# Gate and up projections of the dense layer: seven block products in place of eight for 20 of 22 column tiles

## The reference

```python
def swiglu(hn, w_gu, w_down):
    gte, up = jnp.split(hn @ w_gu, 2, axis=-1)
    return (jax.nn.silu(gte) * up) @ w_down
```

## Time and profile before

| | |
|---|---|
| Median of 3 runs | 1522.55 us (1520.13 to 1527.19) |
| The profiled execution | 1524.27 us, span of its instructions 1522.5 us |
| Granted TensorE clock, mean | 0.966 |
| TensorE busy | 1423.7 us, 94% |
| VectorE busy | 898.6 us, 59% |
| ScalarE busy | 639.4 us, 42% |
| GpSimd busy | 239.1 us, 16% |
| Gate and up of the dense layer | from 458.9 us to 713.4 us |
| Down projection of the dense layer | from 713.4 us to 840.1 us |

### The profile page before, as it was taken

How to read it: one execution, slowest core, us unless ns; L and a number is a source line. 1 busy time by engine, 2 the same in 40 slices (tenths; PEclk the granted TensorE clock), 3 DMA queues, 4 the chain that set the end, 5 groups by cost and what they waited for, 6 DMA issues and landing times. The chain is left out here.

```text
span 1522.5 us, 31277 instructions
## 1 busy us (share of the span) xinstructions
PE 1423.7 (94%) x12955; PEld 1264.7 (83%) x12955; DVE 898.6 (59%) x1196; ACT 639.4 (42%) x1076; POOL 239.1 (16%) x243
## 2 busy tenths in 40 slices
PE   7999999999899999999999997879599999999994
PEld 6999988888799999999999997559566777777772
DVE  5677536865755444444444756553547777677776
ACT  4444534441333222222233522662536556565661
POOL 0111016764120000000111101330140000000002
PEclk8999999999999999999999998899789999999997
DMA  6677422001523323332324540005267888888886
GB/s 185 211 287 264 132 77 52 2 3 31 180 85 107 87 83 100 93 83 70 100 82 133 148 107 32 1 18 150 76 200 257 294 282 294 293 287 274 273 285 236
DMA packets 170201, 226.47 MB, mean 149 GB/s; under 512 B 11544, under 2 KB 135089, under 8 KB 170009
## 3 DMA queue, kind: packets, MB, share of 16 engines
q1 hardware_dynamic: 160246, 191.44, 40.4%
q0 software_dynamic: 8976, 30.88, 5.7%
q10 hardware_dynamic: 862, 2.50, 0.5%
HBM read 188.78 MB, written 38.28 MB: 149 GB/s over the span
## 5 line engine op out<-in xcount | busy, mean ns | idle before, releaser
L281 DVE TENSOR_TENSOR w_lo<-w_raw,w_hi 128x2048 fp32r<-128x2048 f32 (+1 forms) x70 | 151.6, 2171 | 95.7 <-ACT w_hi L273 95.7
L226 PE MATMUL P<-xf_hi,w_hi 128*128 128x260 f32 x704 | 199.0, 283 | 2.0 <-DVEq L1857 1.2
L226 PE MATMUL P<-xf_hi,w_lo 128*128 128x260 f32 x704 | 198.9, 283 | 0.0
L226 PE MATMUL P<-xf_lo,w_hi 128*128 128x260 f32 x704 | 198.3, 282 | 0.0
L273 ACT ACTIVATE w_hi<-w_raw 128x2048 fp32r<-128x2048 f32 (+1 forms) x71 | 128.1, 1810 | 126.2 <-PE P L226 114.7
L226 PE MATMUL P<-xa_hi,w_hi 128*128 128x260 f32 x512 | 146.0, 285 | 5.3 <-DVE xa_lo L324 5.3
L226 PE MATMUL P<-xa_hi,w_lo 128*128 128x260 f32 x512 | 145.8, 285 | 0.0
L226 PE MATMUL P<-xa_lo,w_hi 128*128 128x260 f32 x512 | 145.4, 284 | 0.0
L226 PEld LDWEIGHTS P<-xf_hi,w_hi 128*128 128x128 f32 x704 | 132.5, 188 | 2.6 <-issue 1.4
L226 PEld LDWEIGHTS P<-xf_hi,w_lo 128*128 128x128 f32 x704 | 132.4, 188 | 0.0
L226 PEld LDWEIGHTS P<-xf_lo,w_hi 128*128 128x128 f32 x704 | 132.4, 188 | 0.0
(11 more groups left out here) (562 smaller groups left out, 3421.4 us busy)
## 6 DMA issues: line engine op xcount, KB each, us to landing
raw_more_moe<-in_moe_w_gu_dram SPq DMA_DIRECT2D x64, 512.0 KB, 5.4
w_raw<-in_moe_w_gu_dram SPq DMA_DIRECT2D x64, 512.0 KB, 6.1
w_raw<-in_dense_w_gu_dram SPq DMA_DIRECT2D x44, 512.0 KB, 5.1
expert_out<-zeros POOLq DMA_DIRECT2D x40, 512.0 KB, 4.2
w_raw<-in_a_w_in_dram SPq DMA_DIRECT2D x32, 512.0 KB, 5.0
raw_more_moe<-in_moe_w_down_dram SPq DMA_DIRECT2D x32, 512.0 KB, 4.8
w_raw<-in_moe_w_down_dram SPq DMA_DIRECT2D x32, 512.0 KB, 4.8
w_raw<-in_dense_w_down_dram SPq DMA_DIRECT2D x16, 384.0 KB, 3.9
```

The costliest lines, as they stand in the source:

```text
L226: ins = nc.tensor.matmul(out[:, b], w, x[:, b * HALF:(b + 1) * HALF], start=(first and n == 0), stop=(last and n == 2))
L281: ins = nc.vector.tensor_tensor(lo, raw, hi.bitcast(F32), ALU.subtract)
```

## The change

For tiles 2 to 21 the block product of weights and tokens is made with seven products in place of eight (Winograd's form of Strassen's scheme). The blocks of the weights are: A11 and A12, the gate columns of the first and last four feature blocks, A21 and A22 the same of the up columns. The tokens are split in four too: first and last four feature blocks, first and second half of the tokens. A weight block is 128 x 512. Four of the seven products take sums of weight blocks, S1 = A21 + A22, S2 = S1 - A11, S3 = A21 - A11 and S4 = A12 - S2, and four take sums of token blocks, which are made once. A product is 4 (blocks) x 3 = 12 matmuls of 260 columns in a bank of its own, so a tile takes 84. What each engine now does for a tile:

- GpSimd makes the four sums of the next tile's weights (`sums`), and multiplies `scratch` by `rstd` (`scale_up`).
- ScalarE casts seven pieces of 512 columns to `w_hi` (`high_piece`), each as soon as TensorE has used the same piece of the tile before, and copies the first bank out.
- VectorE makes seven `w_lo` pieces (`low_piece`) and, between them, seven additions of 260 columns that put gate and up together from the banks (`add`).
- Once, at the start: VectorE makes the token sums from `h` (`sum_tokens`), ScalarE their high parts, VectorE their low parts (`low_sum`). The high parts are put where `h` lies, so SyncE writes `h` out to memory first (`h_rows`) and reads it back behind the last product (`restored`), ahead of the rest of the down weights.

The core of the diff:

```diff
+    ORDER = ("A11", "S2", "S3", "S1", "A12", "A22", "S4")
...
         def _(sp):
+            sp.dma_start(h_rows, c.h[:].rearrange("p k t -> p (k t)")).then_inc(spilled, 16)
             st_gu.rest(c, sp)
             st_down.start(c, sp)
+            sp.wait_ge(used, all_used)
+            sp.dma_start(c.h[:].rearrange("p k t -> p (k t)"), h_rows).then_inc(restored, 16)
             st_down.rest(c, sp)
...
+            def sums(i, j):
+                pool.wait_ge(*loaded_of(i, j))
...
+                pool.wait_ge(piece_lo, piece_of(i, j, 3))
+                nc.gpsimd.tensor_tensor(to["S1"], a21, a22, ALU.add).then_inc(sums_made, 1)
+                pool.wait_ge(sums_made, count(1))
+                nc.gpsimd.tensor_tensor(to["S2"], to["S1"], a11, ALU.subtract).then_inc(sums_made, 1)
+                nc.gpsimd.tensor_tensor(a21, a21, a11, ALU.subtract).then_inc(sums_made, 1)
+                pool.wait_ge(sums_made, count(2))
+                pool.wait_ge(piece_lo, piece_of(i, j, 6))
+                nc.gpsimd.tensor_tensor(to["S4"], a12, to["S2"], ALU.subtract).then_inc(sums_made, 1)
+
+            def scale_up(i, j):
+                pool.wait_ge(read, read_of(i, j, 6))
+                nc.gpsimd.tensor_tensor(L.sf[:, j], L.sf[:, j], inward.rstd, ALU.mult).then_inc(up_read, 1)
+
+            sums(0, 1)
+            with pool.Fori(1, NFF // 2 - 1) as i:
+                for j in range(2):
+                    sums(i, j)
+                    scale_up(i, j)
...
+            def seven(i, j, first=False):
+                for q, name in enumerate(sv.ORDER):
+                    pe.wait_ge(piece_lo, piece_of(i, j, q))
...
+                    if q == 0:
+                        pe.wait_ge(first_copied, i * 2 + j)
+                    else:
+                        pe.wait_ge(read, read_of(i, j, (1, 2, 4, 5, 6, 7)[q - 1], -1))
...
+                    for k in range(4):
+                        for n, (w, x) in enumerate(((w_hi, x_hi), (w_hi, x_lo), (w_lo, x_hi))):
+                            ins = pe.matmul(c.P[:, q, 0:HALF], w[:, k], x[:, k], start=(k == 0 and n == 0), stop=(k == 3 and n == 2))
+                    ins.then_inc(used, 1)
...
+            def gu(i, j, last=False):
+                act.wait_ge(used, used_of(i, j, 0))
+                nc.scalar.activation(part(L.sg[:, j], 0), c.P[:, sv.bank("A11"), 0:HALF], ACT.Copy).then_inc(first_copied, 1)
...
+                    for q in range(pieces):
+                        high_piece(i, j, q, (used, used_of(i, j, q)))
+                    chunk_done(i, j)
+                silu(i, j)
+                f_high(i, j)
...
+            def gu(i, j, last=False):
...
+                low(0)
+                dve.wait_ge(first_copied, i * 2 + (j + 1))
+                add(i, j, 1, sv.one, gates[0], bank(1))
+                low(1)
...
+                add(i, j, 2, sv.three, sv.one, bank(2))
+                low(2)
...
+                add(i, j, 3, ups[1], sv.three, bank(3))
+                add(i, j, 3, gates[1], sv.one, bank(3))
+                low(3)
+                add(i, j, 4, gates[0], gates[0], bank(4))
+                low(4)
+                add(i, j, 5, ups[0], sv.three, bank(5))
+                low(5)
...
+                add(i, j, 6, gates[1], gates[1], bank(6))
+                dve.wait_ge(read, read_of(i, j, 7))
+                nc.vector.tensor_tensor(L.sg[:, j], L.sg[:, j], inward.rstd, ALU.mult).then_inc(gate_read, 1)
+                if last:
+                    st_down.split_lo(nc, c, dve, 0, 0)
+                else:
+                    low(6)
+                    chunk_done(i, j)
+                made_f(i, j)
...
+            st_gu.split_lo(nc, c, dve, 0, 1)
+            inward.finish(nc, c, dve, 2)
+            sum_tokens()
+            gate(0)
+            up(0)
+            made_f(0, 0)
+            low_sum(0)
+            low_sum(1)
+            for q in range(4):
+                low_piece(0, 1, q)
+            gate(1)
+            dve.wait_ge(ready, 4)
+            low_sum(2)
+            up(1)
+            low_sum(3)
```

More of the change, by code:

```diff
@@ L1837, in _, with silu, f_high @@
[L1837 to L1841, removed]
+            def silu(i, j):
+                act.wait_ge(gate_read, i * 2 + (j + 3))
+                nc.scalar.activation(L.sg[:, j], L.sg[:, j], ACT.Silu).then_inc(silu_done, 1)
+            def f_high(i, j):
+                act.wait_ge(f_made, i * 2 + (j + 1))
+                nc.scalar.activation(L.f_hi[:, i * 2 + j], L.sf[:, j], ACT.Copy).then_inc(f_hi_ready, 1)
@@ new lines, in _ @@
+            act.sem_inc(piece_hi, 2 * pieces)
+            act.sem_inc(first_copied, 2)
+            st_gu.split_hi(nc, c, act, 0, 1)
+            inward.root(nc, act)
+            silu(0, 0)
+            f_high(0, 0)
+            act.wait_ge(spilled, 16)
+            act.wait_ge(x_sums, 1 + 4 * 4)
+            for n in range(4):
+                nc.scalar.activation(sv.t_hi[n], sv.t_raw[n], ACT.Copy).then_inc(x_sums_hi, 1)
+            for q in range(4):
+                high_piece(0, 1, q, (ready, 2))
@@ L1842, in _ @@
+            silu(0, 1)
+            for q in range(4, pieces):
+                high_piece(0, 1, q, (ready, 4))
+            chunk_done(0, 1)
+            f_high(0, 1)
+            with act.Fori(1, NFF // 2 - 1) as i:
+                for j in range(2):
+                    gu(i, j)
+            gu(NFF // 2 - 1, 0)
+            gu(NFF // 2 - 1, 1, last=True)
+            act.wait_ge(used, all_used)
             for q in range(chunks):
@@ L1861, in _ @@
                 inward.low(nc, c, dve, k)
-            def gu(i, first=False, last=False):
-                for j in range(2):
[L1865 to L1879, removed]
-                                            ALU.subtract).then_inc(f_ready, 1)
@@ new lines, in low_sum @@
+            def low_sum(n):
+                dve.wait_ge(x_sums_hi, n + 1)
+                lo, raw, hi = sv.t_lo[n], sv.t_raw[n], sv.t_hi[n].bitcast(F32)
+                if n == 1:
+                    nc.vector.tensor_tensor(lo.three, raw[:, 0:3], hi[:, 0:3], ALU.subtract)
+                    lo, raw, hi = lo.last, raw[:, 3], hi[:, 3]
+                nc.vector.tensor_tensor(lo, raw, hi, ALU.subtract).then_inc(x_sums_lo, 1)
+            dve.sem_inc(piece_lo, 2 * pieces)
+            dve.sem_inc(read, 21)
@@ L1885, in _ @@
+            made_f(0, 1)
+            with dve.Fori(1, NFF // 2 - 1) as i:
+                for j in range(2):
+                    gu(i, j)
+            gu(NFF // 2 - 1, 0)
+            gu(NFF // 2 - 1, 1, last=True)
+            dve.wait_ge(restored, 16)
             for q in range(chunks):
```

152 lines of the change are left out of this document (132 added, 20 removed).

## The result

The changed kernel takes 1574.88 us (median of 4 executions, 1573.28 to 1577.28), the kernel before 1521.34 (4, 1518.33 to 1527.19): 1.0352 times as long, 95% interval 1.033 to 1.0375. The forecast was 1576. The profiled execution took 1573.28 us, its span is 1571.5.

A forecast was written before the change was run, and what follows sets the result against it. VectorE and GpSimd, excluding each other, were to set a 13.7 us tile: 18 x (13.7 - 11.48) = +40, start and end the rest of +53.6, 1524.3 to 1577.9, less 1.7: 1576 us. Range 1560 to 1600 (0.70), wider 1540 to 1605.

The forecast's parts named there:

- VectorE and GpSimd shut each other out, not TensorE sets the pace: Tiles 2 to 21: GpSimd and two-SBUF-input VectorE instructions take turns, 1.70 us a pair; TensorE's own pace would be 10.05.
- The tile, 13.7 us: One tile on VectorE: 0.5 first piece, five GpSimd pairs 8.5, free additions and pieces 4.6, register instructions 0.1.
- whole durations: Skill's rule that ports are kept for whole instructions: a pair 1.97 us, tile below 15.0, kernel 1600; not followed.
- VectorE alone, 9.8 us: VectorE's work a tile without GpSimd's interference: 8.5 us of instructions, 0.92 idle before `f_lo`, 0.4 for dependent waits.
- The point at which the sign changes, 10.7 us a tile: Tile pace at which the changed kernel would equal the old: (713.4 - 11.2 - 509.2) / 18.
- The start: Ahead of tile 2: token sums, 7.3 us on VectorE, and casts let TensorE start at 492.4, 8.6 us lost.
- The end: From bank 5 of tile 20 at 755.8 through tile 21 and first down split: 11.2 us, down starts 767.0.
- h out and back: Residual's 2.13 MB each way, about 7 us; back issued about 760, landed about 769; costs nothing, 3 us in hand.
- TensorE's share, 0.73: Sign in the changed trace: TensorE's busy share between 510 and 750 us about 0.73, idle 3.6 us a tile.
- the rival of the clock: TensorE's idling in tiles drops its clock to half; if it stayed there, 1657 us; price above 1600 given 0.07.
- The sum: Whole kernel: +53.6 us on 1524.3 gives 1577.9 for the profiled execution; 1.7 above the median, so 1576.
- The lower bound of the tile, 11.25: Ports held 5 x 1.15 us by GpSimd and 10 x 0.55 by VectorE, with every addition hidden.

The follow-up runs named there:

- the shorter products: Changed kernel with two of three products on TensorE in tiles 2 to 21 (56 matmuls instead of 84): 1574.62 us, a tile 13.53 us.

## Why the prediction was right

- **VectorE and GpSimd shut each other out, not TensorE sets the pace:** shown, by leaving the sums out, by memsets in their place, by one sum more and by taking a third off TensorE.
- **The tile, 13.7 us:** 13.56. The five turns were laid out at 5 x 1.70 = 8.5 us; GpSimd's five run from 604.36 to 612.86, 8.5. The free part, from the start of the addition behind piece 0 at 613.33 to the end of the next bank 5 addition at 617.82, is 4.5 (4.6 laid out). Following the measured hand-over rather than whole durations, which gave 15.0, was worth 1.3 us a tile. The pair is shorter than its durations in this trace too: GpSimd's start 1.66, 1.83, 1.59 and 1.69 us apart.
- **VectorE alone, 9.8 us:** about 0.3 too small, by a subtraction and not by a run of its own. Without the sums a tile takes 10.72, of which 0.66 is the gate scaling beside GpSimd's scaling: 10.1. VectorE still waits 0.42 us for the silu in the tile shown; I had hidden that.
- **The point at which the sign changes, 10.7 us a tile:** at 10.72 the kernel stood at 1520.3 against 1522.6.
- **The start:** tile 2 at 491.46 (492.4 forecast), its bank 5 addition at 508.95 (509.2).
- **The end:** down starts at 765.61 (767.0). The tiles brought it 2.8 us earlier, at 752.99 instead of 755.8; the end took 12.6 us where I had laid out 11.2, of which 1.07 is VectorE's wait for TensorE in tile 21.
- **h out and back:** the way back took 8.8 us from issue to landing, about the 9 laid out, but began some 2 us late; landed at 770.9, not 769. VectorE waited 3.35 us for it, TensorE did not.
- **TensorE's share, 0.73:** mis-sized, 0.81. I had its waits at 3.6 us a tile at full clock. From tile 4 on they are 3.2 to 3.3 us in eleven tiles, 1.7 to 1.8 in four and 0.7 to 0.9 in three, because in eight of the tiles the granted clock falls to half for 3.4 or 6.8 us and the matmuls spread over the time there was. Their spacing is then 0.217 us in place of 0.12. The prediction had named changed spacing as a sign of being wrong, and it did change; but the rival of the clock, true in its mechanism, costs nothing here: with a third of TensorE's work gone the tile stays.
- **The sum:** the profiled executions put the start of down at 765.6 against 713.4, +52.2 (+53.6 forecast); the medians differ by 53.5. That the total is met to about 1 us is in part luck. Start and tiles were 2.8 us shorter than laid out and the end 1.4 longer, and the forecast of 1577.9 for the profiled execution was missed by 4.6 us (1573.28), of which 3.2 lie behind the start of down, mostly in stages that the change does not touch and that vary from execution to execution.
- **The lower bound of the tile, 11.25:** it rests on 0.55 us for which VectorE is said to hold its instruction's way to SBUF; no row was given for it, and no run measured it.

## What to carry to other kernels

Work on GpSimd is not free because GpSimd is idle: beside VectorE instructions with two inputs in SBUF each sum cost the tile 0.7 us, more than the 0.6 that it takes on VectorE itself; beside a row of instructions that read PSUM, as long as the work is, three sums cost 0.6 us together. A stretched instruction looks busy, so compare the length of an instruction in both profiles before trusting a busy share. Before taking work off the engine that bounds, lay out one tile on every other engine, and on each pair that shares a way to SBUF: here an eighth fewer matmuls paid only while that tile stayed under 10.7 us. When VectorE is full, look also at which of its instructions frees the next bank, since moving it by one place cost 0.4 us a tile.

## What the runs showed of the hardware

- GpSimd's sum of 128 x 512 has two lengths: 1.26 to 1.31 us beside nothing or beside VectorE instructions with one input in PSUM, 1.62 to 1.75 in turns with VectorE instructions that have two inputs in SBUF. Its memset of the same size takes 0.52, and VectorE's instructions beside it kept 0.68 and 0.70.
- A VectorE instruction that writes PSUM, with one input there, takes 0.42 us for 260 columns and starts 0.34 after the one before, about as one that writes SBUF (0.41), also beside a sum of GpSimd; no run here had one with both inputs in SBUF and its output in PSUM.
- TensorE's clock: with gaps of up to 3.3 us a tile it was granted at half (1.2 GHz) for a part of eight of 18 tiles, from 519.6 us on, for instance, 1 us behind a gap of 3.32, and from 721.0 on, within one of 3.24; through the gaps that end between 613 and 655 us, as long, it stayed at full clock. The granted clock was 0.93 over the stretch, 0.80 with the shorter products. In the versions whose gaps in the tiles are below 1 us it stayed at 2.4 GHz (1.00).
